# Turning P by whole 128-query blocks in a dilated-window attention stage, one unit to a PSUM bank

## The chip, the cores and the metric

The kernel runs on one core of a Trainium2 chip. The metric is the time of one execution in device microseconds. Times of single instructions come from one execution under the hardware profiler. PE is TensorE (PEld its weight loads), DVE VectorE, ACT ScalarE, POOL GpSimd, SP the engine that issues the DMAs here.

## What is computed

One layer of an encoder, on a prompt of 4096 tokens and on one of 2048, all in float32: `x + concat[attn * silu(g_a), fourier * silu(g_f)] @ w_out`, with all branches out of one projection of the normed `x`. The change touches the attention branch alone:

```python
PATTERNS = ((128, 1), (512, 4), (2048, 16))      # window, dilation
...
s = jnp.einsum('brnqhd,brnkhd->brnhqk', qb, kb, preferred_element_type=jnp.float32) * scale + bias
s = jnp.where(mask[:, None], s, NEG)
lse = jax.nn.logsumexp(s, axis=-1)
p = jnp.exp(s - lse[..., None])
o = jnp.einsum('brnhqk,brnkhd->brnqhd', p.astype(vb.dtype), vb, preferred_element_type=jnp.float32)
```

There are 12 heads of 64 channels. Each query sees 64 keys to either side at distances of 1, 4 and 16 tokens; the three results are merged later with weights from their denominators.

## The kernel before, in words

The stages follow each other: two projections (to about 2060 us), the Fourier branch, **attention** (`attention(core)`, 2392 to 3550 us), and `combine`, which merges the three patterns, multiplies by the gates and by `w_out`.

The work unit of attention is a `Unit`: 128 queries of one residue class against up to 256 keys, in two chunks of 128 keys (a class of exactly 128 tokens, in the shorter sequence at dilation 16, has one chunk). There are 144 units a head pair. A step `q` handles two units `i` for both heads `e` of the pair; 72 steps (`PER`) make a pair, and the body of a pair is written out in full and run for 6 pairs, four of them in a hardware loop. PE, ACT, DVE, POOL and SP each have a body of their own, and semaphores join them.

A step goes like this:

- `score` (L1233): for each unit and head three matmuls of 64-row tiles (q and k are held as two parts each), e = 0 on rows 0 to 63, e = 1 on rows 64 to 127, into PSUM `ps_s[q % 2][e]`: 12 matmuls.
- DVE `add_bias` (L1356): adds the bias, negates, takes the minimum, and writes `p[q % 4]`, queries on partitions and keys along the free axis.
- ACT `exponent` (L1297): exp in place, four a step; the fourth raises `exp_done`.
- PE `turn_p` (L1249): P has to stand with keys on partitions for the last product, so each 128x128 block is transposed. Before, each block goes as two halves: queries 0 to 63 (rows 0 to 63 of the array) into `ps_low`, queries 64 to 127 (rows 64 to 127) into `ps_high`, 64 columns each: 16 transposes a step, 8 for a one-chunk step. The last one raises `p_turned`.
- ACT `copy_low` (L1308, L1310) and DVE `copy_high` (L1367, L1369): each copies its bank to SBUF, 128x512, or 128x256 with one chunk. Both wait for `p_turned`.
- PE `weigh` (L1268): P times V, with one column tile for queries 0 to 63 and another for 64 to 127; the trace shows two matmuls for each one written, 32 a step. Into `ps_o[q % 2]`, which DVE (even q) and ACT (odd q) copy out (L1376, L1317).

PE's order is written out by hand. One round, `j`, is two steps:

```python
turn_p(it, 2 * j + 1)
score(it, 2 * j + 3); score(it, 2 * j + 4)
turn_p(it, 2 * j + 2)
weigh(it, 2 * j); weigh(it, 2 * j + 1)
```

So the copies of a turned P lie beside the two scores or beside the two `weigh` that follow. DVE's order in a round is copy of o, `copy_high(2j+1)`, `add_bias(2j+3)`, `copy_high(2j+2)`, `add_bias(2j+4)`; ACT's is the same with `copy_low` and `exponent`. For dilations 1 and 4 POOL packs the queries of a step (L1189) five steps ahead. SP stores the results, loads values and the next pair's q and k in pieces of 256 KB, tied to rounds.

Of the kernel before, what the change touches and what calls it, by code (L numbers as in the profile page):

```python
# [25 lines left out]
P = 128  # L26
D = 1024
HD = 64
# [63 lines left out]
class Core:  # L92
# [5 lines left out]
    def sb(self, stack, name, shape, dt=F32):  # L98
        return stack.enter_context(self.nc.sbuf_tensor(name, shape, dt))
# [942 lines left out]
def attention(core):  # L1042
# [5 lines left out]
    bias_in, cleared = [S(f"bias_in{i}") for i in range(n_d)], S("cleared")  # L1048
    v_in, stored = ([S(f"{n}{i}") for i in range(BUFS)] for n in ("v_in", "stored"))
    scored, biased, exp_done, p_turned = (S(n) for n in ("scored", "biased", "exp_done", "p_turned"))  # L1050
    low_copied, high_copied, pv_done, waited = (S(n) for n in ("low_copied", "high_copied", "pv_done", "waited"))
    packed = S("packed")
    v_cleared, pool_waited = [S(f"v_cleared{i}") for i in range(BUFS)], S("pool_waited")
    w_out_kept, pe_waited, sp_waited = S("w_out_kept"), S("pe_waited"), S("sp_waited")
# [3 lines left out]
    with ExitStack() as st:  # L1058
# [5 lines left out]
        v = [sb(f"v{i}", [P, 24, PW]) for i in range(BUFS)]  # L1064
        o = [sb(f"o{i}", [P, STRETCH, OW]) for i in range(BUFS)]
        p = [sb(f"p{i}", [P, 2, 2, 2 * P]) for i in range(RING)]
        p_low, p_high = ([sb(f"p_{n}{i}", [P, 2, 2, 2, HD]) for i in range(RING)] for n in ("low", "high"))
        ps_s = [[core.ps(st, f"att_ps_s{i}{e}") for e in range(2)] for i in range(2)]
        ps_low, ps_high = core.ps(st, "att_ps_low"), core.ps(st, "att_ps_high")
        ps_o = [core.ps(st, f"att_ps_o{i}") for i in range(2)]  # L1070
        block = st.enter_context(nc.Block())

# [12 lines left out]
        def wait(engine, semaphore, count):  # L1085
            if not isinstance(count, int) or count > 0:
                engine.wait_ge(semaphore, count)
# [128 lines left out]
        @block.tensor  # L1216
        def _(pe):
            def score(it, q):

                if q % PER == 0:  # L1220
                    pe.wait_ge(b_in, pair_of(it, q) * (16 * B_PIECES) + 16 * B_PIECES)
                if q % PER == 24:
                    pe.wait_ge(a_in, pair_of(it, q) * (16 * A_PIECES) + 16 * A_PIECES)
                wait(pe, biased, it * (4 * PER) + 4 * (q - 1))
                if place(q) in loose:
                    pe.wait_ge(packed, it * packs(PER) + packs(q) + 1)
                for i, u in enumerate(two(q)):
                    have = region[parts[place(q)].name]
                    query = u.queries(have[:, 0:2, :]) if u.dil == LANES else q_packed[q % RING][:, i]
                    for n, (x, y) in enumerate(((0, 2), (0, 3), (1, 2))):  # L1230
                        for e in range(2):
                            rows = slice(HD * e, HD * (e + 1))
                            ins = pe.matmul(ps_s[q % 2][e][:, 2 * P * i:2 * P * i + u.w],  # L1233
                                            query[rows, x, :], u.keys(have[rows, y, :]),
                                            start=(n == 0), stop=(n == 2))
                ins.then_inc(scored, 1)

            def turn_p(it, q):

                pe.wait_ge(exp_done, it * PER + (q + 1))  # L1240
                wait(pe, low_copied, it * PER + q)
                wait(pe, high_copied, it * PER + q)
                pe.sem_inc(pe_waited, 1)
                for i, u in enumerate(two(q)):
                    for e in range(2):
                        for j, (at, _, _) in enumerate(u.chunks):
                            for to, lo in ((ps_low, 0), (ps_high, HD)):
                                rows = slice(lo, lo + HD)
                                ins = pe.transpose(to[:, ((2 * i + e) * 2 + j) * HD:((2 * i + e) * 2 + j + 1) * HD],  # L1249
                                                   p[q % RING][rows, i, e, at:at + P], core.ident[rows, rows])  # L1250
                ins.then_inc(p_turned, 1)

            def weigh(it, q):

                n = place(q)
                if q % 8 == 0:
                    wait(pe, v_cleared[n % BUFS], it * each(n_clears, n) + same(n_clears, n) + n_clears[n])
                    pe.wait_ge(v_in[n % BUFS], it * (16 * each(n_loads, n)) + 16 * (same(n_loads, n) + n_loads[n]))
                pe.wait_ge(low_copied, it * PER + (q + 1))
                pe.wait_ge(high_copied, it * PER + (q + 1))  # L1260
                wait(pe, o_copied[q % 2], it * (PER // 2) + q // 2)
                pe.sem_inc(pe_waited, 1)
                for i, u in enumerate(two(q)):
                    for e in range(2):
                        to = i * PW + e * VW
                        for j, (_, chunk, _) in enumerate(u.chunks):
                            for have, lo in ((p_low, 0), (p_high, HD)):
                                ins = pe.matmul(ps_o[q % 2][lo:lo + HD, to:to + VW], have[q % RING][:, i, e, j, :],  # L1268
                                                v[n % BUFS][:, chunk, e * VW:(e + 1) * VW],
                                                start=(j == 0), stop=(j == len(u.chunks) - 1))  # L1270
                ins.then_inc(pv_done, 1)

            def body(it, more):
                for j in range(PER // 2):
                    turn_p(it, 2 * j + 1)
                    for h in range(2):
                        if here(it, more, 2 * j + 3 + h):
                            score(it, 2 * j + 3 + h)
                    if here(it, more, 2 * j + 2):
                        turn_p(it, 2 * j + 2)  # L1280
                    for h in range(2):
                        weigh(it, 2 * j + h)

            for q in range(3):
                score(0, q)
            pe.wait_ge(cleared, RING)
            turn_p(0, 0)
            pairs(pe, body)

        @block.scalar  # L1290
        def _(act):
# [6 lines left out]
                if (i, e) == (1, 1):  # L1298
                    ins.then_inc(exp_done, 1)

            def copy_low(it, q):

                act.wait_ge(p_turned, it * PER + (q + 1))
                wait(act, pv_done, it * PER + (q - RING + 1))
                have = ps_low[:].rearrange("p (i e j c) -> p i e j c", i=2, e=2, j=2)
                n = len(two(q)[0].chunks)
                if n == 2:
                    ins = act.activation(p_low[q % RING][:], have, ACT.Copy)  # L1308
                else:
                    ins = act.activation(p_low[q % RING][:, :, :, 0, :], have[:, :, :, 0, :], ACT.Copy)  # L1310
                ins.then_inc(low_copied, 1)

            def copy_o(it, q):

# [5 lines left out]
            def body(it, more):  # L1320
                for j in range(PER // 2):
                    if here(it, more, 2 * j - 1):
                        copy_o(it, 2 * j - 1)
                    for h in range(2):
                        q, t = 2 * j + 3 + h, 2 * j + 1 + h
                        if here(it, more, t):
                            copy_low(it, t)
                        if here(it, more, q):
                            for i in range(2):
                                for e in range(2):  # L1330
                                    exponent(it, q, i, e)

            for q in range(3):
                for i in range(2):
                    for e in range(2):
                        exponent(0, q, i, e)
            copy_low(0, 0)
            pairs(act, body)
            copy_o(PAIRS - 1, PER - 1)

# [1 line left out]
        def _(dve):  # L1342
# [14 lines left out]
                                             bias[:, u.d, e, u.lo:u.lo + u.w], -1.0, -3 * NEG, ALU.add, ALU.min,  # L1357
                                             o[n % BUFS][:, (2 * q + i) % STRETCH, PW + e:PW + e + 1]).then_inc(biased, 1)

            def copy_high(it, q):  # L1360

                dve.wait_ge(p_turned, it * PER + (q + 1))
                wait(dve, pv_done, it * PER + (q - RING + 1))
                have = ps_high[:].rearrange("p (i e j c) -> p i e j c", i=2, e=2, j=2)
                n = len(two(q)[0].chunks)
                if n == 2:
                    ins = dve.tensor_copy(p_high[q % RING][:], have)  # L1367
                else:
                    ins = dve.tensor_copy(p_high[q % RING][:, :, :, 0, :], have[:, :, :, 0, :])  # L1369
                ins.then_inc(high_copied, 1)  # L1370

            def copy_o(it, q):

# [5 lines left out]
            def body(it, more):  # L1379
                for j in range(PER // 2):  # L1380
                    if here(it, more, 2 * j - 2):
                        copy_o(it, 2 * j - 2)
                    for h in range(2):
                        q, t = 2 * j + 3 + h, 2 * j + 1 + h
                        if here(it, more, t):
                            copy_high(it, t)
                        if here(it, more, q):
                            add_bias(it, q, 0)
                            add_bias(it, q, 1)

            dve.wait_ge(cleared, RING)
            for q in range(3):
                for i in range(2):
                    add_bias(0, q, i)
            copy_high(0, 0)
            pairs(dve, body)
            copy_o(PAIRS - 1, PER - 2)

# [254 lines left out]
```

## Time and profile before

| | |
|---|---|
| Time, median of 3 runs | 4155.04 us (4154.98 to 4171.92) |
| The profiled execution | 4166.38 us |
| Its span | 4164.6 us |
| Granted clock of TensorE, mean | 0.962 |
| Attention stage (2392 to 3550 us) | 1158 us |
| PE busy over the span | 3798.7 us, 91% |
| DVE, ACT, POOL busy over the span | 61%, 41%, 10% |

In the timeline each row is: start in us from the span's start, length in us, engine, line, operation, what it writes and reads, shape, count; in brackets the idle time of the engine before it and what ended it. Matmuls are pipelined, so one lasts longer than the time from its start to the next start, and it is the starts that count. "issue" means that the engine waited for nothing the profile shows.

### The profile page before, as it was taken

The page shows a single profiled execution, that of the slowest core. Times are in us where ns is not written, and L with a number is a line of the kernel's source. Part 1 is how long each engine was busy: PE and PEld are TensorE (multiplying, and loading weights), DVE is VectorE, ACT ScalarE, POOL GpSimd, SP SyncE. Part 2 cuts the span into 40 slices and gives each one's busy share as a digit, 9 for nine tenths or more (in the row PEclk, how much of TensorE's full clock was granted, in tenths as well). Part 3 has the DMA queues.
Part 4 walks back from the last instruction along what each step waited for, and adds up shares of the span by engine and source line. Part 5 has one row for each costly group of instructions (what it writes and reads, how often), then busy time and mean ns, then how long its engine had stood idle before and what let it go on. Part 6 is the DMA issues. An engine that isn't in the chain of part 4 may idle for free. (4 is left out here: it accounts for less than half of the span.)

```text
span 4164.6 us, 105562 instructions
## 1 busy us (share of the span) xinstructions
PE 3798.7 (91%) x38254; PEld 3242.0 (78%) x38254; DVE 2552.7 (61%) x7710; ACT 1687.9 (41%) x4443; POOL 400.8 (10%) x674
## 2 busy tenths in 40 slices
PE   3599999999979999999987589889988899799999
PEld 2588888888868888888872378888888888688887
DVE  3366666666646445454442268778777788777775
ACT  2233333333322111111111178878877788433332
POOL 0000000000000000000000133324242432000000
PEclk7799999999999999999996799999999999899999
DMA  6444434443547544444549976666757575566664
GB/s 130 122 141 169 147 132 155 155 149 131 172 148 220 173 145 145 146 144 141 147 122 263 245 229 179 173 170 174 193 149 191 142 202 136 206 249 237 243 243 180
DMA packets 604204, 722.38 MB, mean 173 GB/s; under 512 B 37215, under 2 KB 473567, under 8 KB 602112
## 3 DMA queue, kind: packets, MB, share of 16 engines
q1 hardware_dynamic: 603840, 717.55, 57.8%
q8 instruction: 226, 3.70, 0.4%
q14 instruction: 138, 1.13, 0.1%
HBM read 383.67 MB, written 337.94 MB: 173 GB/s over the span
## 5 line engine op out<-in xcount | busy, mean ns | idle before, releaser
L474 PE MATMUL p_ps<-p_w_hi,p_h_hi 128*128 128x512 f32 (+1 forms) x3072 | 1144.9, 373 | 22.3 <-DVE p_w_lo L756 20.9
L474 PE MATMUL p_ps<-p_w_lo,p_h_hi 128*128 128x512 f32 (+1 forms) x3072 | 1123.5, 366 | 0.0
L474 PE MATMUL p_ps<-p_w_hi,p_h_lo 128*128 128x512 f32 (+1 forms) x3072 | 1123.0, 366 | 0.0
L1297 ACT ACTIVATE att_p<-att_p,att_o 128x256 f32<-128x256 f32 (+2 forms) x1728 | 683.4, 467 | 203.5 <-DVE att_o L1356 202.0
L474 PEld LDWEIGHTS p_ps<-p_w_hi,p_h_hi 128*128 128x128 f32 x3072 | 582.1, 189 | 116.6 <-issue 18.4
L474 PEld LDWEIGHTS p_ps<-p_w_hi,p_h_lo 128*128 128x128 f32 x3072 | 581.5, 189 | 97.2
L474 PEld LDWEIGHTS p_ps<-p_w_lo,p_h_hi 128*128 128x128 f32 x3072 | 582.5, 190 | 92.2
L1356 DVE CUSTOM_DVE_ANT_0 att_p<-att_ps_s,att_bias 128x256 f32<-128x256 f32 (+2 forms) x1728 | 560.6, 381 | 142.2 <-PE att_ps_s L1233 142.2
L1268 PE MATMUL att_ps_o<-att_v,att_p_low 128*64 128x65 f32 x6528 | 435.3, 225 | 10.6 <-issue 8.8
L1268 PE MATMUL att_ps_o<-att_v,att_p_high 128*64 128x65 f32 x6528 | 435.8, 225 | 3.4 <-issue 3.4
L1268 PEld LDWEIGHTS att_ps_o<-att_v,att_p_low 128*64 128x64 f32 x6528 | 403.1, 139 | 23.3 <-issue 8.4
L1268 PEld LDWEIGHTS att_ps_o<-att_v,att_p_high 128*64 128x64 f32 x6528 | 403.2, 139 | 7.8 <-issue 7.7
L1367 DVE COPY att_p_high<-att_ps_high 128x512 f32<-128x512 f32 x384 | 264.8, 690 | 116.9 <-PE att_ps_high L1249 114.0
L711 DVE RECIPROCAL p_denom<-p_denom 128x256 f32<-128x256 f32 x144 | 329.2, 2286 | 4.9
L709 DVE TENSOR_SCALAR p_denom<-p_expo 128x256 f32<-128x256 f32 x144 | 48.7, 338 | 444.3 <-ACT p_expo L588 444.3
L1249 PE MATMUL att_ps_low<-ident,att_p 64*128 64x64 f32 x3264 | 290.4, 228 | 26.4 <-issue 19.6
L1500 PE MATMUL out_ps_y<-out_w_hi,out_m_hi 128*128 128x512 f32 x768 | 308.7, 402 | 2.3 <-DVE out_m_lo L1600 2.3
L1500 PE MATMUL out_ps_y<-out_w_hi,out_m_lo 128*128 128x512 f32 x768 | 304.3, 396 | 0.0
L1500 PE MATMUL out_ps_y<-out_w_lo,out_m_hi 128*128 128x512 f32 x768 | 304.2, 396 | 0.0
L1249 PE MATMUL att_ps_high<-ident,att_p 64*128 64x64 f32 x3264 | 292.0, 229 | 5.0 <-issue 5.0
L1249 PEld LDWEIGHTS att_ps_low<-ident,att_p 64*128 64x128 f32 x3264 | 247.3, 141 | 43.0 <-issue 27.2
L677 DVE TENSOR_REDUCE p_sumsq<-p_squares 128x8 f32<-128x512 f32 x144 | 98.8, 686 | 291.1 <-ACT p_squares L553 291.1
(111 smaller groups left out, 5104.4 us busy)
## 6 DMA issues: line engine op xcount, KB each, us to landing
scratch_qk<-p_staging SPq DMA_DIRECT2D x72, 1024.0 KB, 5.6
out_o<-scratch_o SPq DMA_DIRECT2D x144, 396.0 KB, 5.4
att_qk_a<-scratch_qk SPq DMA_DIRECT2D x192, 256.0 KB, 4.3
scratch_o<-att_o SPq DMA_DIRECT2D x168, 264.0 KB, 3.3
p_x<-x SPq DMA_DIRECT2D x48, 512.0 KB, 4.6
scratch_h_t<-p_h_hi SPq DMA_DIRECT2D x48, 512.0 KB, 5.5
scratch_h_t<-p_h_lo SPq DMA_DIRECT2D x48, 512.0 KB, 6.4
p_h_hi<-scratch_h_t SPq DMA_DIRECT2D x48, 512.0 KB, 3.9
```

The costliest lines, as they stand in the source:

```text
L474: ins = pe.matmul(ps[c][:, 0:width[c]], a[s][:, k, :], b[:, k, cols], start=(k == 0 and n == 0), stop=(k == KC - 1 and n == 2))
L677: dve.tensor_reduce(sumsq[:], squares[:].rearrange("p (h w) -> p h w", w=HD), AX.X, ALU.add).then_inc(chain, 1)
L709: dve.tensor_scalar(denom[:, w], expo[:, w], 1.0, None, ALU.add).then_inc(chain, 1)
L711: dve.reciprocal(denom[:, w], denom[:, w]).then_inc(chain, 1)
L1249: ins = pe.transpose(to[:, ((2 * i + e) * 2 + j) * HD:((2 * i + e) * 2 + j + 1) * HD], p[q % RING][rows, i, e, at:at + P], core.ident[rows ...
L1268: ins = pe.matmul(ps_o[q % 2][lo:lo + HD, to:to + VW], have[q % RING][:, i, e, j, :], v[n % BUFS][:, chunk, e * VW:(e + 1) * VW], start=(j ...
L1297: ins = act.activation(at, at, ACT.Exp, bias=o[n % BUFS][:, (2 * q + i) % STRETCH, PW + e:PW + e + 1], scale=-1.0)
L1356: dve.tensor_tensor_reduce(p[q % RING][:, i, e, 0:u.w], ps_s[q % 2][e][:, 2 * P * i:2 * P * i + u.w], bias[:, u.d, e, u.lo:u.lo + u.w], -1 ...
L1367: ins = dve.tensor_copy(p_high[q % RING][:], have)
L1500: ins = pe.matmul(ps_y[2 * s + c][:], a[s][:, k, :], b[:, k, c * BANK:(c + 1) * BANK], start=(k == 0 and n == 0), stop=(k == KC - 1 and n ...
```

## The change

`turn_p` transposes each 128x128 block of P in one instruction on all 128 rows, with 128 columns. Unit 0 of the step goes into bank `ps_p[0]`, unit 1 into `ps_p[1]`, so 8 transposes a step instead of 16. ACT now copies unit 0's bank (`copy_even`), DVE unit 1's (`copy_odd`), with the same element counts as before. `weigh` keeps its matmuls and takes queries `lo` to `lo + 64` out of the unit's own tile. The order on all engines and all the waits stay, with the semaphores renamed.

```diff
-        p_low, p_high = ([sb(f"p_{n}{i}", [P, 2, 2, 2, HD]) for i in range(RING)] for n in ("low", "high"))
+        p_t = [[sb(f"p_t{n}{i}", [P, 2, 2, P]) for i in range(RING)] for n in range(2)]
...
-        ps_low, ps_high = core.ps(st, "att_ps_low"), core.ps(st, "att_ps_high")
+        ps_p = [core.ps(st, f"att_ps_p{i}") for i in range(2)]
...
-                            for to, lo in ((ps_low, 0), (ps_high, HD)):
-                                rows = slice(lo, lo + HD)
-                                ins = pe.transpose(to[:, ((2 * i + e) * 2 + j) * HD:((2 * i + e) * 2 + j + 1) * HD],
-                                                   p[q % RING][rows, i, e, at:at + P], core.ident[rows, rows])
+                            ins = pe.transpose(ps_p[i][:, (2 * e + j) * P:(2 * e + j + 1) * P],
+                                               p[q % RING][:, i, e, at:at + P], core.ident[:])
                 ins.then_inc(p_turned, 1)
...
-                            for have, lo in ((p_low, 0), (p_high, HD)):
-                                ins = pe.matmul(ps_o[q % 2][lo:lo + HD, to:to + VW], have[q % RING][:, i, e, j, :],
+                            for lo in (0, HD):
+                                ins = pe.matmul(ps_o[q % 2][lo:lo + HD, to:to + VW], p_t[i][q % RING][:, e, j, lo:lo + HD],
...
-                have = ps_low[:].rearrange("p (i e j c) -> p i e j c", i=2, e=2, j=2)
+                have = ps_p[0][:].rearrange("p (e j c) -> p e j c", e=2, j=2)
                 n = len(two(q)[0].chunks)
                 if n == 2:
-                    ins = act.activation(p_low[q % RING][:], have, ACT.Copy)
+                    ins = act.activation(p_t[0][q % RING][:], have, ACT.Copy)
...
-                have = ps_high[:].rearrange("p (i e j c) -> p i e j c", i=2, e=2, j=2)
+                have = ps_p[1][:].rearrange("p (e j c) -> p e j c", e=2, j=2)
                 n = len(two(q)[0].chunks)
                 if n == 2:
-                    ins = dve.tensor_copy(p_high[q % RING][:], have)
+                    ins = dve.tensor_copy(p_t[1][q % RING][:], have)
```

## Rows read from the trace of the kernel before

**Rows 1.** Busy time by stretch: length, engines (instructions), PE clock, DMA share, GB/s
```profile
2392.00:3550.00 1158.00, 1035.21 (x24738) 977.92 (x24734) 890.70 (x4090) 933.71 (x2371) 376.65 (x646) 0.98 0.66 175
...
2603.54:2608.34 4.80, 4.80 (x124) 4.62 (x120) 4.47 (x22) 4.57 (x13) 2.44 (x4) 1.00 0.98 300
```

**Rows 2.** Timeline of PE, one round of attention, from 2600.99
```profile
2600.99 0.22 PE L1249 MATMUL att_ps_low<-ident,att_p 64*128 64x64 f32 x1
...
2601.37 0.22 PE L1249 MATMUL att_ps_low<-ident,att_p 64*128 64x64 f32 x1
...
2601.53 0.27 PE L1268 MATMUL att_ps_o<-att_v,att_p_low 128*64 128x65 f32 x1
...
2603.39 0.22 PE L1268 MATMUL att_ps_o<-att_v,att_p_low 128*64 128x65 f32 x1
...
2603.54 0.27 PE L1249 MATMUL att_ps_low<-ident,att_p 64*128 64x64 f32 x1
...
2603.66 0.22 PE L1249 MATMUL att_ps_low<-ident,att_p 64*128 64x64 f32 x1
...
2604.03 0.22 PE L1249 MATMUL att_ps_low<-ident,att_p 64*128 64x64 f32 x1
...
2604.06 1.69 PE L1233 MATMUL att_ps_s<-qk_b,att_q 64*128 64x256 f32 x24
```

**Rows 3.** Costliest groups, the transposes on rows 0 to 63
```profile
L1249 PE MATMUL att_ps_low<-ident,att_p 64*128 64x64 f32 x3264 | 290.4, 228 | 26.4 <-issue 19.6
```

**Rows 4.** Waits in attention, weight loads by "issue": us, times, longest
```profile
PEld att_ps_s L1233 <- issue: 78.6, 83, 3.6
...
PEld att_ps_low L1249 <- issue: 27.2, 31, 4.5
...
PEld att_ps_o L1268 <- issue: 16.1, 19, 1.7
...
PEld att_ps_high L1249 <- issue: 9.9, 8, 2.1
```

**Rows 5.** Timeline of PE and its weight loads: three of the stalls
```profile
3090.91 1.18 PE L1233 MATMUL att_ps_s<-att_qk_a,att_q 64*128 64x256 f32 x14 [1.73 <-issue]
...
3127.00 0.81 PE L1233 MATMUL att_ps_s<-att_qk_a 64*128 64x192 f32 x11 [1.75 <-issue]
...
2792.70 0.14 PEld L1249 LDWEIGHTS att_ps_low<-ident,att_p 64*128 64x128 f32 x1 [4.50 <-issue]
```

**Rows 6.** Busy time of PE from stall to stall (matmuls), clock, DMA share, GB/s
```profile
3090.90:3096.63 5.73, 5.05 (x121) 1.00 0.65 162
...
3120.36:3127.00 6.64, 4.89 (x122) 1.00 0.71 164
```

**Rows 7.** DMA queues: the queue that brings instructions, whole span
```profile
q8 instruction: 226, 3.70, 0.4%
```

**Rows 8.** Timeline of PE in the last stage: eight full-width transposes
```profile
3804.69 1.04 PE L1487 MATMUL out_ps_t<-ident,out_mix 128*128 128x128 f32 x8
3805.48 0.48 PE L1500 MATMUL out_ps_y<-out_w_hi,out_m_hi 128*128 128x512 f32 x1
```

**Rows 9.** Lines L1487 and L1249: least, median, greatest length in ns
```profile
L1487 PEld LDWEIGHTS out_ps_t<-ident,out_mix x384: 138/141/231, 3568.8 to 4143.6; 128*128 128x128 f32 x192
L1487 PE MATMUL out_ps_t<-ident,out_mix x384: 270/272/473, 3568.8 to 4143.7; 128*128 128x128 f32 x192
...
L1249 PEld LDWEIGHTS att_ps_low<-ident,att_p x3264: 134/139/223, 2392.1 to 3547.4; 64*128 64x128 f32 x192
```

**Rows 10.** Waits in attention on other engines
```profile
POOL att_q L1189 <- DMA att_qk_a<-scratch_qk: 52.9, 6, 10.9
...
PE att_ps_s L1233 <- POOL att_q L1189: 13.8, 6, 3.4
...
PE att_ps_s L1233 <- DVE att_o L1356: 10.2, 10, 1.6
```

**Rows 11.** Costliest groups, DVE's copy of a turned P
```profile
L1367 DVE COPY att_p_high<-att_ps_high 128x512 f32<-128x512 f32 x384 | 264.8, 690 | 116.9 <-PE att_ps_high L1249 114.0
```

**Rows 12.** Granted clock of PE in 40 slices of 104 us, tenths
```profile
PEclk7799999999999999999996799999999999899999
```

More of the change, by code:

```diff
@@ L1050, in attention @@
     scored, biased, exp_done, p_turned = (S(n) for n in ("scored", "biased", "exp_done", "p_turned"))
-    low_copied, high_copied, pv_done, waited = (S(n) for n in ("low_copied", "high_copied", "pv_done", "waited"))
+    even_copied, odd_copied, pv_done, waited = (S(n) for n in ("even_copied", "odd_copied", "pv_done", "waited"))
     packed = S("packed")
@@ L1240, in turn_p @@
                 pe.wait_ge(exp_done, it * PER + (q + 1))
-                wait(pe, low_copied, it * PER + q)
-                wait(pe, high_copied, it * PER + q)
+                wait(pe, even_copied, it * PER + q)
+                wait(pe, odd_copied, it * PER + q)
                 pe.sem_inc(pe_waited, 1)
@@ L1258, in weigh @@
                     pe.wait_ge(v_in[n % BUFS], it * (16 * each(n_loads, n)) + 16 * (same(n_loads, n) + n_loads[n]))
-                pe.wait_ge(low_copied, it * PER + (q + 1))
-                pe.wait_ge(high_copied, it * PER + (q + 1))
+                pe.wait_ge(even_copied, it * PER + (q + 1))
+                pe.wait_ge(odd_copied, it * PER + (q + 1))
                 wait(pe, o_copied[q % 2], it * (PER // 2) + q // 2)
@@ L1299, in exponent, with copy_even @@
                     ins.then_inc(exp_done, 1)
-            def copy_low(it, q):
+            def copy_even(it, q):
                 act.wait_ge(p_turned, it * PER + (q + 1))
                 wait(act, pv_done, it * PER + (q - RING + 1))
-                have = ps_low[:].rearrange("p (i e j c) -> p i e j c", i=2, e=2, j=2)
+                have = ps_p[0][:].rearrange("p (e j c) -> p e j c", e=2, j=2)
                 n = len(two(q)[0].chunks)
                 if n == 2:
-                    ins = act.activation(p_low[q % RING][:], have, ACT.Copy)
+                    ins = act.activation(p_t[0][q % RING][:], have, ACT.Copy)
                 else:
-                    ins = act.activation(p_low[q % RING][:, :, :, 0, :], have[:, :, :, 0, :], ACT.Copy)
-                ins.then_inc(low_copied, 1)
+                    ins = act.activation(p_t[0][q % RING][:, :, 0, :], have[:, :, 0, :], ACT.Copy)
+                ins.then_inc(even_copied, 1)
             def copy_o(it, q):
@@ L1326, in body @@
                         if here(it, more, t):
-                            copy_low(it, t)
+                            copy_even(it, t)
                         if here(it, more, q):
@@ L1336, in _ @@
                         exponent(0, q, i, e)
-            copy_low(0, 0)
+            copy_even(0, 0)
             pairs(act, body)
@@ L1358, in add_bias, with copy_odd @@
                                              o[n % BUFS][:, (2 * q + i) % STRETCH, PW + e:PW + e + 1]).then_inc(biased, 1)
-            def copy_high(it, q):
+            def copy_odd(it, q):
                 dve.wait_ge(p_turned, it * PER + (q + 1))
                 wait(dve, pv_done, it * PER + (q - RING + 1))
-                have = ps_high[:].rearrange("p (i e j c) -> p i e j c", i=2, e=2, j=2)
+                have = ps_p[1][:].rearrange("p (e j c) -> p e j c", e=2, j=2)
                 n = len(two(q)[0].chunks)
                 if n == 2:
-                    ins = dve.tensor_copy(p_high[q % RING][:], have)
+                    ins = dve.tensor_copy(p_t[1][q % RING][:], have)
                 else:
-                    ins = dve.tensor_copy(p_high[q % RING][:, :, :, 0, :], have[:, :, :, 0, :])
-                ins.then_inc(high_copied, 1)
+                    ins = dve.tensor_copy(p_t[1][q % RING][:, :, 0, :], have[:, :, 0, :])
+                ins.then_inc(odd_copied, 1)
             def copy_o(it, q):
@@ L1385, in body @@
                         if here(it, more, t):
-                            copy_high(it, t)
+                            copy_odd(it, t)
                         if here(it, more, q):
@@ L1394, in _ @@
                     add_bias(0, q, i)
-            copy_high(0, 0)
+            copy_odd(0, 0)
             pairs(dve, body)
```

## Prediction

> **What bounds the kernel now.** I read the split of the span by stage first. The change touches the attention stage alone, which runs from 2392 to 3550 us: 1158 us, in which PE is busy for 1035, ACT for 934, DVE for 891 and POOL for 377, while the DMA engines are used to 0.66 [rows 1]. Its work is 6 head pairs of 36 rounds, 216 rounds of two steps q each, so 5.36 us a round. One round without any stall, 2603.54 to 2608.34, lasts 4.80 us; PE is busy for all of it, DVE for 4.47 and ACT for 4.57 [rows 1]. So PE sets the pace and the two copying engines are 5 to 7% behind it: PE time added is paid in full, PE time saved would be worth a quarter of a microsecond a round at most.
>
> Next, the order of starts on PE in that round. A transpose on row tile 0-63 and its twin on 64-127 start within 0.01 us of each other, and the next pair follows after 0.05 to 0.06 us: from 2600.99 to 2601.37 there are six steps, 0.063 us each, and there are 3264 such pairs [rows 2, 3]. The two row tiles thus work beside each other.
>
> Last, where PE stands still. In the waits of the weight loads "issue", time in which nothing that is shown was waited for, holds 78.6 + 27.2 + 16.1 + 9.9 = 131.8 us [rows 4]. It comes in a pattern: such stalls end at 3090.91 and 3127.00, with more between them [rows 5], and the stretches from one such end to the next, of which two are shown, hold 121 and 122 matmuls [rows 6]; a full round has 32 transposes, 24 score matmuls and 64 of P times V, 120. The instruction queue moved 226 packets, 3.70 MB, 16.4 KB each [rows 7]. I read this as PE waiting for its own program: a block of instructions worth one full round arrives in 5.73 to 6.64 us here, where the work in it takes about 5. The Trainium skill, page "Runtime: NRT & Kernel Launch", section Instruction fetch mechanics, says that instructions come in blocks of 16 KiB, 256 of them, and that crossing a block is mostly hidden. The size agrees with the packets; "mostly hidden" doesn't hold in these stretches.
>
> **The change, part by part.**
> 1. *Width of a transpose.* A pair of 64-row transposes with 64 moving columns each becomes one 128-row transpose with 128 moving columns. The same form stands in the last stage: eight in a row, 3804.69 to an end 1.04 us later, where one lasts 0.27 (the merged row and the median); so seven steps in 0.77 us, 0.110 us each [rows 8, 9]. Weight loads have the same length in both forms (medians 141 and 139 ns) [rows 9], so the moving columns make the difference. Cost: 3264 x (0.110 - 0.063) = +153 us. Pipelining at the ends of a phase trims a little (a phase of eight takes 0.37 more, two a round, over 192 full rounds and half that in the 24 rounds with one chunk: +150). I take **+145**, with bounds 135 and 155.
> 2. *Changes of tile shape.* Before, score and transposes both use 64-row tiles: the score's first matmul starts 0.03 us after the last transpose (2604.03 to 2604.06). From transposes to P times V, 64x128 tiles to 128x64, it is 0.16 us (2601.37 to 2601.53), back again 0.15 (2603.39 to 2603.54), and the first step after it is 0.12 instead of 0.06 [rows 2]. A change of shape thus costs about 0.09 + 0.05. After the change the borders score-transposes and transposes-score become changes too, two new ones a round. No row shows 64x128 beside 128x128; bounds are 0 (it drains nothing) and 0.15 each. I take 0.09, for the last score matmul and the last full-width transpose already last longer than a 64-column one: 216 x 2 x 0.09 = **+40 us**, bounds 0 and 65. The Trainium skill, page "TensorEngine Tiling (Array Packing)", section Key Properties, says that a change of tiling mode drains TensorE, and a change of tile doesn't. By the rule the two new borders cost what the old two do, +60; without it part 2 is nothing. The old borders agree with it.
> 3. *Fewer instructions.* Of 120 matmuls with their loads a round 16 go: 104/120 of the stream. A block that held one round now holds 1.15 rounds, or 1.15 x (4.80 + 0.75 + 0.18) = 6.6 us of work. The two intervals shown, 5.73 and 6.64 [rows 6], are no longer than that, so the fetch falls behind the work almost everywhere. Of the 131.8 us of issue waits some stand at the loop's jump back from one pair to the next (4.50 us before the first transpose of one) [rows 5] and stay: four such jumps at 4.2 or so, 17 us. Refundable: 115. I take **-108**; bounds -118 and, if a stall is a fixed price of crossing a block, 115 x 16/120 = -15.
> 4. *Waits on others.* PE waits 13.8 us for POOL's packed queries and 10.2 for DVE, and POOL in turn waits 52.9 us for loads of q and k to land [rows 10]. A slower PE gives all of them time: **-10**, bounds 0 and -24.
> 5. *Copies.* ACT and DVE each still copy one bank of 128x512 a step, 0.69 us on DVE [rows 11]; in the one-chunk steps 256 elements. Same sizes, same engines, nothing. They can't start sooner: p_turned is still raised once, after both banks, so the first unit's full bank waits for the second's. The later p_turned is covered: a copy is needed only after the two scores or the two P times V that follow, 1.5 us or more [rows 2]. If that cover were gone it would cost the copy's 0.69 us a step. No DMA, no POOL work and no queue is moved.
>
> P times V reads the same 64 columns from another address; nothing. **Sum:** +145 + 40 - 108 - 10 = **+67 us**. The profiled execution took 4166.4 us by the clock of the runs, its span is 4164.6; with the sum, 4233. The median of the runs is 4155.0, 11 below, so I forecast 4222 for the median, 1.6% slower.
>
> **Rivals.**
> *The change of shape is free* (part 2 at 0, part 3 and 4 at their best): 145 - 118 - 20 = +7, 4162 to 4185, no change to speak of. For it: no row has this border. Against: the two borders that rows do have. 0.12.
> *A full-width transpose costs what a pair does.* This is the one that ends faster. If the 0.063 us of a pair is set by loading 128 columns of weights, a full-width one takes 0.063 too; part 1 is 0, the round needs 4.98 us, and fewer instructions help: 0 + 40 - 118 x 0.7 - 0 = -43 us, 4112. It decides as soon as the step is under about 0.085 us, where part 1 is 72 and the sum near 0. Against it: eight full-width transposes at 0.110 us, with the same load time [rows 8, 9]. 0.05.
> *The stalls stay.* If the stall is tied to the crossing and not to how far the fetch has come: 145 + 40 - 15 - 10 = +160, 4315. For it: stalls of 1.7 us in stretches where DMA is used to only 0.65 and 0.71 [rows 5, 6]. Against: the round from 2603.54 has none [rows 1], and holds a block's worth of instructions too. 0.11.
> *The clock.* Transposes rise from 3264 x 0.063 = 206 of 1158 us to 3264 x 0.110 = 359 of 1225, from 18 to 29% of the stage. Its granted clock is 0.98, and the slices inside it show 9, where the two just before it show 6 and 7 [rows 1, 12]. If it fell to 0.90, 1200 us of work would take 1333 instead of 1224: 67 + 109 more, 4331. The Trainium skill, page "TensorE: Matmul & The Clock Gate", section Part 4: PE-mode transpose, says that transposes don't count as activity for the full clock. Against it: the stage is 18% transposes already and has 0.98. 0.05.
>
> **How the numbers follow.** Forecast 0.67 (4190 to 4265), free change of shape 0.12, cheap transpose 0.05, stalls stay 0.11, clock 0.05. Half a per cent, 21 us, is about what a measurement of this kernel can tell from no change: "same" is 4134 to 4176. Faster is the cheap transpose, 0.05. Same is most of the free change of shape, 0.10. Slower is the rest, 0.85. The range holds the forecast and the free change of shape and reaches some way towards the stalls that stay: 4170 to 4282.
>
> **What would show it.** Right: PE's transposes x3264 instead of 6528, 0.110 us from start to start; score's first matmul 0.15 us or more behind the last transpose; a round without stall of 5.6 to 5.8 us; issue waits of the loads down from 132 to 15 to 35 us; the stage 1215 to 1240 us and all other stages unchanged; DVE and ACT wait longer for PE. Wrong: a step near 0.06 (the refund then carries the sign), issue waits still near 100, or a stage clock under 0.95.

## The result, and the profile after

The changed kernel takes 4239.1 us (median of 4 runs, 4231.2 to 4245.4) against 4155.0 (4 runs, 4145.5 to 4171.9): ratio 1.0197, interval 1.0158 to 1.0236, so **2.0% slower**. Forecast were 4222 and a range of 4170 to 4282. The profiled executions differ by 64.8 us in span (4164.6 to 4229.4), where the sum said 67. Two executions among the experiments, one of 8861 us (the kernel before with 96 columns) and one of 15739 us (the odd steps), stand far outside all others and enter no ratio.

Busy time by stretch, after: before attention, attention, and behind it (length, PE, PEld, DVE, ACT, POOL, clock, DMA share, GB/s):

```profile
0.00:2387.00 2387.00, 2173.65 (x10835) 1787.10 (x10836) 1213.86 (x2750) 539.74 (x1346) 24.31 (x29) 0.95 0.53 159
2387.00:3615.00 1228.00, 1200.30 (x21468) 1082.28 (x21468) 902.90 (x4088) 958.99 (x2370) 373.51 (x646) 0.99 0.62 165
3615.00:4229.40 614.40, 585.76 (x2688) 474.63 (x2688) 448.42 (x872) 214.19 (x728) 0.00 (x0) 0.98 0.63 229
```

The stage grew by 70 us against [rows 1], from 1158 to 1228; the last stage has its 614 us as before, and the 2392 us ahead of it became 2387, which the change doesn't touch. DVE and ACT do the same work as before: their busy times, 903 and 959 us from 891 and 934, count overlapping instructions once, and by their single instructions ACT's copy of a turned P takes 590 ns from 584, DVE's 691 from 690. PE goes from 1035 busy out of 1158 to 1200 out of 1228: it is now nearly without a gap, and slower all the same. Its clock is 0.99.

One round of PE after (its timeline, merged rows):

```profile
2609.94 1.72 PE L1233 MATMUL att_ps_s<-qk_b,att_q 64*128 64x256 f32 x24
2611.59 1.09 PE L1247 MATMUL att_ps_p<-ident,att_p 128*128 128x128 f32 x8
2612.61 2.09 PE L1266 MATMUL att_ps_o<-att_v,att_p_t 128*64 128x65 f32 x64
2614.63 1.09 PE L1247 MATMUL att_ps_p<-ident,att_p 128*128 128x128 f32 x8
2615.65 1.65 PE L1233 MATMUL att_ps_s<-qk_b,att_q 64*128 64x256 f32 x24
2617.23 1.09 PE L1247 MATMUL att_ps_p<-ident,att_p 128*128 128x128 f32 x8
2618.26 2.09 PE L1266 MATMUL att_ps_o<-att_v,att_p_t 128*64 128x65 f32 x64
```

The round, 2612.61 to 2618.26, is 5.65 us. Eight transposes hold PE for 1.02 us until the next kind starts, whichever it is. In [rows 2] the phase before the scores held it for 0.52 (2603.54 to 2604.06), the one before P times V for 0.59, from this row to 2601.53:

```profile
2600.94 0.22 PE L1249 MATMUL att_ps_low<-ident,att_p 64*128 64x64 f32 x1
```

The last transpose starts at 2614.63 + 1.09 - 0.27 = 2615.45, the first score at 2615.65: 0.20 us, where it was 0.03 [rows 2].

PE's own waits for "issue" in attention, before and after (us in total, times, longest):

```profile
PE att_ps_s L1233 <- issue: 52.1, 65, 1.7
PE att_ps_low L1249 <- issue: 19.6, 10, 4.4
...
PE att_ps_o L1268 <- issue: 12.1, 17, 1.6
...
PE att_ps_high L1249 <- issue: 5.0, 7, 2.0
```
```profile
PEld att_ps_s L1233 <- issue: 41.6, 215, 4.5
PEld att_ps_o L1266 <- issue: 36.1, 216, 0.3
PEld att_ps_p L1247 <- issue: 31.3, 76, 5.3
PE att_ps_p L1247 <- issue: 15.6, 4, 5.2
```

On PE it falls from 88.8 us to 15.6, four waits in all: three of 4.9 to 5.2 us, at the loop's jumps back from one pair to the next, and one of 0.4 us in the first pair. The weight loads still show 109 us, but of another kind: 215 and 216 waits, one a round in each group, the 216 of them 0.17 us each. They belong to the changes of tile shape: in the second experiment, where P times V has the shape of the transposes, the 216 of P times V are gone and those of the scores stay. The instruction queue moved 25 packets less, for 6528 instructions less, 261 to a packet:

```profile
q8 instruction: 201, 3.29, 0.3%
```

### The profile page after: what moved, and what is told of

Read it like the earlier page. It is cut to its first block and busy times, and to the rows that moved or that the text cites. A ratio compares the mean times of both kernels' runs of the same rounds, so it can differ in the third digit from the quotient of the medians.

```text
span 4229.4 us, 99034 instructions
## 1 busy us (share of the span) xinstructions
PE 3959.7 (94%) x34990; PEld 3344.0 (79%) x34990; DVE 2565.2 (61%) x7710; ACT 1712.9 (40%) x4443; POOL 397.8 (9%) x674
## 5 line engine op out<-in xcount | busy, mean ns | idle before, releaser
L1247 PE MATMUL att_ps_p<-ident,att_p 128*128 128x128 f32 x3264 | 455.4, 282 | 17.8 <-issue 15.6
L1266 PE MATMUL att_ps_o<-att_v,att_p_t 128*64 128x65 f32 x13056 | 429.0, 223 | 0.0
L1266 PEld LDWEIGHTS att_ps_o<-att_v,att_p_t 128*64 128x64 f32 x13056 | 399.0, 138 | 36.1 <-issue 36.1
L1247 PEld LDWEIGHTS att_ps_p<-ident,att_p 128*128 128x128 f32 x3264 | 353.1, 142 | 62.6 <-issue 31.3
L1365 DVE COPY att_p_t<-att_ps_p 128x512 f32<-128x512 f32 x384 | 265.4, 691 | 197.8 <-PE att_ps_p L1247 195.2
L553 ACT ACTIVATE p_squares<-p_ps 128x512 f32<-128x512 f32 x144 | 86.0, 597 | 451.6 <-PE p_ps L474 451.6
L588 ACT ACTIVATE p_expo<-p_ps 128x256 f32<-128x256 f32 x144 | 65.4, 454 | 448.4 <-PE p_ps L474 224.7
L1189 POOL CAST att_q<-att_qk_a 128x256 fp32r<-128x256 f32 x384 | 227.4, 644 | 155.9 <-PE att_ps_s L1233 96.0
```

The source lines that it names most:

```text
L553: act.activation(squares[:], ps[c][:], ACT.Square).then_inc(sq_done, 1)
L588: act.activation(expo[:, lo:width[c]], ps[c][:, lo:width[c]], ACT.Exp, scale=-1.0).then_inc(expo_done, 1)
L1189: ins = pool.tensor_copy(q_packed[q % RING][:, i].rearrange("p x (j s) -> p x j s", s=LANES // u.dil), u.queries(region[name][:, 0:2, :]))
L1247: ins = pe.transpose(ps_p[i][:, (2 * e + j) * P:(2 * e + j + 1) * P], p[q % RING][:, i, e, at:at + P], core.ident[:])
L1266: ins = pe.matmul(ps_o[q % 2][lo:lo + HD, to:to + VW], p_t[i][q % RING][:, e, j, lo:lo + HD], v[n % BUFS][:, chunk, e * VW:(e + 1) * VW], ...
L1365: ins = dve.tensor_copy(p_t[1][q % RING][:], have)
```

## The experiments

What the stalls wait for stands in the trace of the kernel before. Of PE's 99 waits on "issue" in attention, 98 end 1.15 to 1.95 us (median 1.43) behind the landing of a packet of the instruction queue, taken as its start plus its duration; of moments spread evenly over the stage 14% would. So PE stands until a piece of its program has come. What is open before the experiments is what a stall depends on.

Theory A: PE is held up by its own instruction stream, which comes at a rate that the work of a round outruns; slower work or fewer instructions lets it catch up. Theory B: every block crossed costs its stall. Spans are those of the profiled executions; ratios are to the kernel before, run again on the same chip beside them (medians 4177 to 4189 there).

**P times V on 128 queries at a time, transposes as before** (both copies write one tile `p_t[..., 0:64]` and `[..., 64:128]`):

```diff
-                            for have, lo in ((p_low, 0), (p_high, HD)):
-                                ins = pe.matmul(ps_o[q % 2][lo:lo + HD, to:to + VW], have[q % RING][:, i, e, j, :],
...
+                            ins = pe.matmul(ps_o[q % 2][:, to:to + VW], p_t[q % RING][:, i, e, j, :],
...
```

> The kernel before, its transposes by halves kept, but both copies write into one tile, and P times V takes all 128 queries as one stationary block: 32 matmuls a round instead of 64 (16 of 120 weight-load and matmul pairs more go than in the change), each over the same 65 columns. Theory A (PE waits for a stream of instructions that arrives at a rate of one block of 256 in 5.2 to 6.7 us): a round needs some 190 entries, the stalls vanish, PE's own work stays near 4.8 us a round if a full-width matmul starts every 0.058 to 0.063 us: 85 to 115 us faster than before, 4040 to 4070. Theory B (each block crossed costs its stall, whatever the pace): a quarter of the crossings go, about 28 us, less 10 to 20 for the slower step: within 20 us of before. Theory C (two column tiles beside each other are what makes P times V fast, a full-width one takes 0.11 like the transposes): 0.05 x 6528 = +340 less the refund, over 200 us slower.

Measured: 4385.6 us, ratio 1.0481 (1.0455 to 1.0507). Theory C was the nearest: a full-width step takes 0.11 us, like a transpose, where a pair of column tiles takes 0.058. That two tiles side by side are worth a factor of two holds for this matmul as well. PE's issue waits are down to 11.9 us here, but with 32 of 120 matmuls gone and the work longer, this can't tell A from B.

**The same in the changed kernel** (`p_t[i][q % RING][:, e, j, :]` as the stationary operand, output on all partitions):

> The changed kernel with P times V on all 128 queries as well. Transposes and P times V then have the same tile shape, so two of the four changes of shape a round are gone; the changed kernel has hardly any stalls left to refund. If a change of shape costs 0.14 us: 216 x 2 x 0.14 = 60 us faster than the changed kernel, less up to 28 us if the full-width step is 0.063 instead of 0.058: 4180 to 4210. If the changes of shape cost nothing and the 0.20 us steps come from something else (the waits before them): 0 to 28 us slower than the changed kernel, 4239 to 4267.

Measured: 4508.1 us, ratio 1.0784 (1.0756 to 1.0811), 269 us over the changed kernel: both expectations were far too low, since both took the step at 0.063. But its timeline answers the question about shapes. A phase of transposes ahead of P times V, and one ahead of the scores:

```profile
3162.27 1.04 PE L1247 MATMUL att_ps_p<-ident,att_p 128*128 128x128 f32 x8
3163.24 1.72 PE L1233 MATMUL att_ps_s<-qk_b,att_q 64*128 64x256 f32 x24
3164.89 1.09 PE L1247 MATMUL att_ps_p<-ident,att_p 128*128 128x128 f32 x8
3165.82 2.34 PE L1265 MATMUL att_ps_o<-att_v,att_p_t 128*128 128x65 f32 x20
```

Where transposes and P times V have one shape, 128x128, eight transposes hold PE for 0.93 us (3164.89 to 3165.82) instead of 1.02, with the same waits in the code. So the 0.09 is the change of shape and no semaphore. Entered from the same shape, the phase ahead of the scores is 0.97 instead of 1.02: the first step after a change costs another 0.05.

**Half the change: full width in the even steps** (`if q % 2 == 0:` around the new transpose and the new slice in `weigh`, halves otherwise), and later the same again beside the odd steps:

> Half the change: full-width transposes in the even steps only, halves on row tiles in the odd ones. PE's work rises by half of what the change adds, about 0.52 us a round (108 us), and 8 of 120 matmuls go. If the refund were in proportion to the instructions removed, the sum would be half of the change's, +33 to +42. Theory A (fetch at a rate): a block then holds 5.4 to 5.8 us of work, longer than most fetches, so nearly all of the refund (110 to 145 us) comes with half of the change: -30 to +5 against before, 4125 to 4160.

> The version with full-width transposes in the even steps again, beside the odd one on the same chip: 0.5 to 0.95% faster than before, and within 0.3% of the odd one.

> Half the change, in the odd steps: there the full-width transposes stand between P times V and the scores. One new change of shape a round as with the even steps, and the same 8 matmuls fewer. Theory A: the same as with the even steps, 20 to 35 us faster than before on the same chip.

Measured: even 4155.0, 0.9927 (0.9905 to 0.9949), and again 4160.5, 0.9955 (0.9934 to 0.9977); odd 4155.5, 0.9935 (0.9912 to 0.9958). All three are faster than before, by 0.4 to 0.7%, and even and odd can't be told apart. Half the change doesn't cost half of 2%: it adds half the work and gets nearly all the stalls back. The repeat fell just short of the 0.5% expected. PE's issue waits with the even steps are down to 16.8 us:

```profile
PE att_ps_low L1255 <- issue: 10.5, 3, 3.6
PE att_ps_s L1233 <- issue: 2.6, 3, 1.8
PE att_ps_high L1255 <- issue: 1.2, 1, 1.2
PE att_ps_o L1279 <- issue: 1.0, 3, 0.6
PE att_ps_low L1250 <- issue: 0.9, 5, 0.2
PE att_ps_high L1250 <- issue: 0.6, 1, 0.6
```

**Sixteen more instructions a round, without work** (eight `pe.sem_inc(padded, 1)` ahead of each turn, in the kernel before):

> The kernel before with 16 additions to an unused semaphore a round put into PE's stream, 8 ahead of each turn: no work for the array, 6% more instructions. Theory A: where the fetch is the bound each round becomes 6% longer and more rounds come to be bound by it: 40 to 70 us slower, 4195 to 4225, with the waits on issue up by about that. Theory B: 13 more crossings of 0.5 us on average, 7 us. The additions themselves may cost something between 0 and 20 ns each, up to 70 us, which must then show as longer rounds also where no stall is.

Measured: 4420.5, 1.056 (1.0534 to 1.0586). That is far over the 40 to 70 us of A and the 7 of B, and inconclusive: the additions cost too much themselves. Ahead of a turn PE stands idle for 0.58 to 0.79 us, 0.07 to 0.10 for each addition:

```profile
3161.36 0.24 PE L1251 MATMUL att_ps_low<-ident,att_p 64*128 64x64 f32 x1 [0.79 <-issue]
3163.75 0.24 PE L1251 MATMUL att_ps_low<-ident,att_p 64*128 64x64 f32 x1 [0.58 <-issue]
```

**Slower work with the same instructions.** P times V over 96 columns, in the kernel before and in the changed one:

```diff
-                                ins = pe.matmul(ps_o[q % 2][lo:lo + HD, to:to + VW], have[q % RING][:, i, e, j, :],
-                                                v[n % BUFS][:, chunk, e * VW:(e + 1) * VW],
+                                ins = pe.matmul(ps_o[q % 2][lo:lo + HD, to:to + MOVED], have[q % RING][:, i, e, j, :],
+                                                v[n % BUFS][:, chunk, e * (PW - MOVED):e * (PW - MOVED) + MOVED],
...
```

The 31 further columns belong to the other head; the copies out of `ps_o` leave them and take as many elements as before.

> The kernel before with P times V over 96 columns instead of 65: the further columns are the other head's and are not copied out. Same instructions, same count; only each of the 6528 pairs of column-tile matmuls lasts longer, 0.086 instead of 0.058 us if it goes with the columns: +176 us of array work. Theory A (instructions arrive at a rate, a slower array lets them catch up): the 110 to 145 us of stalls vanish though no instruction was removed, so only 30 to 70 us slower than before. Theory B (a stall belongs to each block crossed): the stalls stay, 165 to 180 us slower.

> The changed kernel with the same 96 columns. It has no stalls left to give back, so by theory A the whole array work shows: 170 to 180 us slower than the changed kernel, against 30 to 70 for the same edit on the kernel before. By theory B both edits cost the same.

Measured: before with 96 columns 4239.3, 1.0138 (1.0101 to 1.0174); the changed kernel with them 4387.2, 1.0487 (1.0456 to 1.0519). The work added is the same. The phase of 64 in the second one:

```profile
3100.77 2.86 PE L1267 MATMUL att_ps_o<-att_v,att_p_t 128*64 128x96 f32 x64
3103.56 1.09 PE L1248 MATMUL att_ps_p<-ident,att_p 128*128 128x128 f32 x8
```

2.86 instead of 2.09 us, +0.77 a full round and half of it in the 24 one-chunk rounds: 192 x 0.77 + 24 x 0.39 = 157 us, a little under the 170 to 180 expected. The changed kernel pays all of it (span 4229.4 to 4385.1, +155.7). The kernel before pays 67 (4164.6 to 4231.6; by medians on its chip 62): 90 us came back, with not one instruction fewer. This is the experiment that tells A from B, for A. Of the 90, 52 are PE's issue waits, 37.0 us from 88.8, which slack in the other engines can't explain; some 14 are its waits for them, and the rest stands in no wait:

```profile
PE att_ps_s L1234 <- issue: 21.2, 35, 1.5
...
PE att_ps_low L1250 <- issue: 11.3, 8, 3.3
PE att_ps_high L1250 <- issue: 2.8, 4, 1.2
...
PE att_ps_o L1269 <- issue: 1.7, 3, 1.2
```

The count of instruction packets is that of before, 226:

```profile
q8 instruction: 226, 3.70, 0.4%
```

**What sets the 0.109 us of a transpose, and the 0.11 of a full-width P times V.** First: ahead of each full transpose one with only 96 keys as the stationary operand (`for keys in (96, P):`). Second: the full-width P times V over 96 columns.

> The changed kernel with a further transpose ahead of each one: the same block with only 96 of its 128 keys as the stationary operand, the same 128 moving columns; the full one then writes the same values again. What limits a full-width transpose? If the moving columns do (the prediction's part 1): from start to start 0.109 us for both kinds, 3264 x 0.109 = +356 us, near 4595. If the weight load does: the narrow one goes with its 96 columns, 0.082, and the sum is about 90 us less, near 4505.

> The second experiment (P times V on all 128 queries, 0.112 us a step) with 96 moving columns instead of 65. If the load of 128 weight columns is what makes the step 0.112: no change, 4500 to 4515. If the moving columns do: 0.112 x 96/65 = 0.165, 0.053 x 6528 = +346 us, near 4850.

Measured in one execution each: 4570.1 and 4496.0. In the first, sixteen steps, half of them with 96 stationary columns:

```profile
3007.89 1.95 PE L1248 MATMUL att_ps_p<-ident,att_p 128*96 128x128 f32 x16
3009.77 2.09 PE L1267 MATMUL att_ps_o<-att_v,att_p_t 128*64 128x65 f32 x64
```

(1.95 - 0.27) / 15 = 0.112 us, the first step's 0.05 in it; the spans differ by 338.9 us (4229.4 to 4568.3), 0.104 for each added one. The narrow loads are shorter (127 ns in the mean against 142), and the steps aren't: **the load doesn't set a transpose.** The moving columns are what is left, and their price fits: P times V by column tiles takes 0.083 us a step with 96 of them ((2.79 - 0.14) / 32, the change of shape taken off), and 0.083 x 128/96 = 0.111. In the second, half as many columns again change nothing (4494.2 of span against 4504.5): **the moving columns don't set the full-width P times V.** That its load does is not shown: no run varied it, and in the kernel before 128 columns are loaded into each row tile every 0.063 us. One floor of about 0.11 us for every full-width step, whatever it loads or moves, would fit all these rows too.

**A quarter of the change** (`q % 4 == 0`), and the whole one again on the same chip:

> A quarter of the change: full-width transposes in every fourth step. Array work rises by 0.26 us a round (54 us), 4 of 120 matmuls go. Theory A: the work of a block grows from about 4.9 to 5.2 us, still shorter than the slower fetches (5.7 to 6.6), so part of the stalls stays: 10 to 40 us faster than before, and not more than the half change by over 0.2%. Theory B: +16 us.

> The changed kernel itself once more, on the chip of the quarter change, so that both stand against the same runs of before. 1.2 to 2.2% slower than before.

Measured: quarter **4126.3 us, 0.9873 (0.9849 to 0.9897)**; the whole change 4241.4, 1.0143 (1.012 to 1.0167). The quarter is 1.3% faster than before and the fastest of all versions. It gains 54 us where 10 to 40 were expected, and its lead over the half, 0.5 to 0.8% by the ratios, is more than the 0.2% allowed. PE's issue waits:

```profile
PE att_ps_low L1255 <- issue: 16.3, 16, 4.1
PE att_ps_s L1233 <- issue: 12.0, 11, 2.3
...
PE att_ps_o L1279 <- issue: 5.7, 9, 1.2
...
PE att_ps_low L1250 <- issue: 2.6, 3, 1.2
...
PE att_ps_high L1255 <- issue: 1.1, 2, 0.9
```

37.7 us: of the 73 above the 16 that the whole change leaves, 70% went, for a quarter of the work. Why so small a slackening of the pace is enough is open. The traces say this much: a packet of 16 KB takes 1.05 to 1.09 us (medians) from its start to its end before, with the quarter and with the half, while one starts every 5.5, 5.5 and 5.8 us. So the stream isn't held up by the transfer itself; what delays the start of the next packet wasn't measured. Theory A is thus shown in that the stalls depend on the pace of the work, and not in that blocks come at one fixed rate.

## Why the prediction was right

The sign, the size and the range held. By its own parts:

1. *Width of a transpose, +145.* Right. The step is 0.109 us as in [rows 8]: 3264 x (0.109 - 0.063) = 150. Its reason, the moving columns, was argued from equal load times; the narrow load has now ruled out the load.
2. *Changes of shape, +40.* The mis-sized term. A change costs 0.09 before and 0.05 behind it also at the new borders, 0.14 in all: 216 x 2 x 0.14 = 60. The prediction had read both figures at the old borders and took the 0.09 alone. The excuse for a lower price, that the last transpose is long anyway, was wrong: the 0.20 us stand between starts where the step itself is 0.11. The Trainium skill, page "TensorEngine Tiling (Array Packing)", section Key Properties, says that a change of tiling mode drains TensorE. The trace agrees at the new borders, with 0.20 us instead of 0.11.
3. and 4. *Refund of the stalls, -108, and of the waits, -10.* Right in kind, too small together: with 150 + 60 of work and +70 for the stage, 140 us came back, not 118. On PE the issue waits shrank by 73, its waits for POOL, DVE and ACT from 32 to 10:

```profile
PE att_ps_s L1233 <- POOL att_q L1189: 7.6, 5, 4.3
...
PE att_ps_p L1247 <- ACT att_p_t L1306: 1.9, 1, 1.9
PE att_ps_s L1233 <- DVE att_o L1354: 0.9, 1, 0.9
```

   Those are 95. The other 45 were never idle time: of PE's 1158 - 1035 = 123 us idle before, its rows list 121, and its busy time grew by 165 us where the added work is 210. They lie in steps that start late while the earlier ones still count as busy, and the prediction's refund was made of listed waits alone. The round of 4.80 us that the prediction took to be free of stalls has some of them:

```profile
2605.62 0.25 PE L1249 MATMUL att_ps_low<-ident,att_p 64*128 64x64 f32 x1
...
2606.26 0.27 PE L1268 MATMUL att_ps_o<-att_v,att_p_low 128*64 128x65 f32 x1
...
2608.34 0.27 PE L1249 MATMUL att_ps_low<-ident,att_p 64*128 64x64 f32 x1
```

   Transposes ahead of P times V hold PE for 0.64 us here and P times V for 2.08, where the round before has 0.59 and 2.01. So a round without late steps was shorter than 4.80 by 0.12 us at least, and the change took more from it than 5.65 - 4.80 says. The two errors, 20 too little cost and 22 too little refund, cancelled. That the sum was within 3 us is therefore partly luck. The waits meant to stay were mis-sized too: the prediction had four jumps and 17 us; the traces show three, of 12 us in all before and 15 after. And its comparison of two intervals was loose, since 6.64 is not below the 6.6 us of work in a block.
5. *Copies, nothing.* Right; DVE's copy is 691 ns, from 690 [rows 11]:

```profile
L1365 DVE COPY att_p_t<-att_ps_p 128x512 f32<-128x512 f32 x384 | 265.4, 691 | 197.8 <-PE att_ps_p L1247 195.2
```

   DVE now waits 195 us for the transposes, from 114 [rows 11]: it idles because PE is late.

Of the signs named, the step, the 0.20 us behind the last transpose, the round of 5.65 and the stage of 1228 came as said. The sign named for the refund was half wrong: the issue waits of the weight loads were to fall to 15 to 35 us and are 109, because waits at the changes of shape are booked there too. PE's own rows would have been the ones to name. The rivals: the free change of shape and the cheap transpose fall with the timeline, the stalls that stay with the 96 columns, the clock with 0.99.

The measured difference of medians, 84 us, is more than the 65 of the spans. The kernel before is the one that moves: its medians beside the experiments, on other chips, were 4177 to 4189, where the changed kernel repeated at 4241 after 4239. The second ratio, 1.0143, is lower for that reason. That fits a kernel which waits for its instructions, but no run was made to show it.

## What to carry to other kernels

When an engine stalls once in a fixed number of its instructions, waiting for nothing that is shown, look whether it waits for its program, by the packets of the instruction queue. If it does, as here, work that needs fewer instructions is cheaper than its busy time says, and even work that is merely slower costs less than it takes (67 us for 157). Before such a trade price both sides, and try it in a part of the steps: all of it was 1.4 to 2.0% slower here, half 0.4 to 0.7% faster, a quarter 1.3% faster. And don't fold two half tiles into one full one for its looks: in these float32 matmuls two row tiles or two column tiles beside each other do in 0.06 us what the full array does in 0.11. Each border between phases of different shape adds 0.14.

## What the runs showed of the hardware that was not expected

- 90 us came back when the array was given 157 us more work, 52 of them in PE's issue waits, with the same 105562 instructions executed.
- 98 of 99 such waits ended 1.15 to 1.95 us behind the landing of an instruction packet, though a packet takes only 1.05 us and one starts every 5.5.
- A full-width P times V takes 0.11 us a step with 65 and with 96 moving columns, a full-width transpose 0.109 with 128 stationary ones and no less with 96 in every other step. The first isn't bound by its moving columns, the second not by its load.
- Behind eight additions to a semaphore in a row PE stood idle for 0.58 to 0.79 us, 0.07 to 0.10 for each, while the single one ahead of P times V costs nothing that can be seen: eight transposes at 0.109 and the 0.05 of a first step make 0.92, and with it they hold PE for 0.93, where the shape stays.
